# Reordering the first loads, transposes and parameter turns of a one-core encoder layer

## The chip, the cores and the metric

The kernel runs on one core of a Trainium2 chip. The metric is device microseconds of one execution, median of the runs shown. The engines are TensorE (PE, with its weight loads as PEld), VectorE (DVE), ScalarE (ACT), GpSimd (POOL) and SyncE (SP, which here only issues DMAs). ACT also has a DMA queue of its own; the rows call the issuing side of the two queues SPq and ACTq.

## What is computed

Two sequences (512 tokens of width 1024 each) go through one encoder layer with shared weights, in float32:

```python
h = rmsnorm(x, norm1) @ w_in            # 1024 -> 256 + 128 + 32 + 512
# latent attention from the first 416 columns, multi-scale pooling from the last 512
x = x + concat(attn, pool) @ w_out
x = x + (silu(gate) * val) @ w_down     # gate, val = dwconv3(rmsnorm(x, norm2) @ w_up)
x = x + (p @ w_ple_proj) * sigmoid(rmsnorm(x, norm3) @ w_ple_gate + b_ple_gate)
y = rmsnorm(x, final_norm)
```

Only the start of the first line, the input projection, bears on this change.

## The kernel before

Every float32 product is made of three reduced-precision matmuls (`mm3`, L313 to L317): a value v is split into a high part (v rounded) and a low part (v minus the high part), and high by high, high by low and low by high are summed in a PSUM bank. Splitting costs an ACT copy for the high part and a DVE subtraction for the low part, for weights (`split_w_hi` L347 on ACT, `split_w_lo` L353 on DVE) as for activations.

The program is five instruction streams written by hand, one for each engine, tied by semaphores. An engine does its stream in order, so a wait in it holds up all that stands behind.

**The head.** x lies in memory by token and must be turned so that features lie on partitions. SP loads it in eight pieces of 512 KB (`load_x(s, q)`, L420: sequence s, 256 columns, that is features of two units). A unit u is 128 features of one sequence, 16 in all, eight for each sequence; piece q of sequence 0 holds units 2q and 2q + 1. For each unit:

- PE (`x_unit`, L694) makes four 128x128 transposes into one of five PSUM banks (`x_bank`), and counts `x_tr`. From unit 5 on it first waits until unit u - 5 has been read out of its bank.
- ACT (`x_unit`, L1268) writes the high part, scaled by the norm1 gain (L1273, tile XH). For units 1, 3, 5, 7 and 9 (`ACT_TURNED`) it first copies the plain turned x to XT (L1272).
- DVE makes the plain copy of the other eleven units (`x_turned`, L1872) and the low part of all (`x_low`, L1878, tile XL), and counts `x_split`.

The norm1 gain is itself loaded as eight rows (`prow[..., 3, :]`, L1255, ACT's first DMA), turned by one PE transpose (L739, waits for the identity matrix and for norm1) and copied to `par` by DVE (L1865); ACT and DVE need it for every unit. Then PE does eight transposes of the identity into a bank that nobody reads (`unread`, L744), units 0 to 3, 18 more unread transposes, and unit 4.

The weight of the projection is loaded in tiles of 128 columns (`first_in`, `load_in`; WR), whose first tile is also rearranged by two POOL instructions (L2636, L2638) before ACT splits it. With the first tile split, PE runs two loops of eight steps, one for each sequence: step k is the three matmuls of `in_tile(0, s, [k])`, which need low parts up to unit 8s + k, and in the first loop and in three steps of the second also four transposes of a later unit. Steps of the first loop carry units 5 to 12, those of the second 13 to 15. After that the second weight tile is used, whose low part (`split_w_lo(dve, 1, 1)`, L1897) DVE makes after its last `x_low`.

Eleven more small loads (conv taps and bias of 44 rows, gains of 1 to 8 rows) fill `prow`; ACT issues all of them at its very start, ahead of its first activation (L1286, which brings its table load). PE turns them in three transposes (L753, L754, L757) after unit 4, before the first loop; DVE copies them to `par` (L1891, L1892) between units 7 and 8.

Of the kernel before, what the change touches and what calls it, by code (L numbers as in the profile page):

```python
# [25 lines left out]
P = 128  # L26
# [3 lines left out]
KT = D // P  # L30
# [13 lines left out]
N1 = 4 * 2 * FT  # L44
N2, N3, GQ = N1 + KT, N1 + 2 * KT, N1 + 3 * KT
GKV, PSC, BG = GQ + 2, GQ + 3, GQ + 7
NF = BG + KT
NPAR = NF + KT
# [24 lines left out]
ACT_TURNED = (1, 3, 5, 7, 9)  # L73
# [16 lines left out]
def encoder(nc, x, p_in, w, y, consts):  # L90
    with ExitStack() as ctx:
        def sb(name, shape, dt=F32):
            return ctx.enter_context(nc.sbuf_tensor(name, shape, dt))

        def sem(name):
            return ctx.enter_context(nc.semaphore(name))


        par = sb("par", [P, LINE * -(-NPAR // LINE)])
# [6 lines left out]
        ident = sb("ident", [P, P])  # L106
# [22 lines left out]
        prow = XT[:, 4096 - 512:4096].rearrange("p (a d) -> p a d", a=4)  # L129
# [59 lines left out]
        def up_w(v, k):  # L189
# [29 lines left out]
        ps = [ctx.enter_context(nc.psum_tensor(f"ps{b}", [P, 512], F32)) for b in range(8)]  # L219
# [7 lines left out]
        ident_in, norm1_in, gains_in, taps_in, tabs_in, edge_in, row_in = (sem(n) for n in (  # L227
            "ident_in", "norm1_in", "gains_in", "taps_in", "tabs_in", "edge_in", "row_in"))
# [12 lines left out]
        w_hi, w_lo, rot_done = sem("w_hi"), sem("w_lo"), sem("rot_done")  # L241
        consts_set, par_tr, par_copied = sem("consts_set"), sem("par_tr"), sem("par_copied")
# [38 lines left out]
        def slot(n):  # L281
            return (n if n < T_GATE else n + 1) % 2
# [10 lines left out]
        def x_bank(u):  # L293

            return ps[(4, 5, 6, 2, 3)[u % 5]]
# [17 lines left out]
        def mm3(pe, out, wh, wl, xh, xl, first, last, skip=False):  # L313

            pe.matmul(out, wh, xh, start=first, stop=False, skip_group_check=skip)  # L315
            pe.matmul(out, wh, xl, start=False, stop=False, skip_group_check=skip)  # L316
            return pe.matmul(out, wl, xh, start=False, stop=last, skip_group_check=skip)  # L317
# [29 lines left out]
        def split_w_hi(act, n, free, count, cols=KT, base=0):  # L347

            if free is not None:
                act.wait_ge(free, count)  # L350
            act.activation(WH[:, slot(n), base:cols, :], WR[:, slot(n), base:cols, :], ACT.Copy).then_inc(w_hi, 1)  # L351
# [59 lines left out]
        def wtile(v):  # L411
            return v.rearrange("(k p) m -> p k m", p=P)
# [1 line left out]

        @block.sync
        def _(sp):
            sp.dma_start(ident[:, :], consts["ident"]).then_inc(ident_in, 16)
            cols_in = [320, 256, 416 + 3 * P, 416 + 2 * P, 416 + P, 0, None, 128, 416]

            def load_x(s, q):  # L420
                cols = slice(q * 2 * P, (q + 1) * 2 * P)
                sp.dma_start(xtok[s][:, :, cols], x[s].rearrange("(t p) d -> p t d", p=P)[:, :, cols]).then_inc(x_in[s * TT + q], 16)

            def first_in(n):
                sp.dma_start(WR[:, n, :, :], wtile(w["w_in"][:, cols_in[n]:cols_in[n] + P])).then_inc(win_in[n], 16)

            load_x(0, 0)
            load_x(0, 1)
            first_in(0)
            load_x(0, 2)  # L430
            load_x(0, 3)
            load_x(1, 0)
# [252 lines left out]
        def _(pe):  # L685
            def x_unit(u):

                s, f = divmod(u, KT)
                pe.wait_ge(x_in[s * TT + f // 2], 16)
                if u >= 5:  # L690
                    pe.wait_ge(x_split, u - 4)
                b = x_bank(u)
                for t in range(TT):
                    ins = pe.transpose(b[:, t * P:(t + 1) * P], xtok[s][:, t, f * P:(f + 1) * P], ident[:, :])  # L694
                ins.then_inc(x_tr, 1)

            def in_tile(a, s, kts=range(KT), fresh=False):
                n = a + (a >= T_POOL)
                for k in kts:
                    if fresh:  # L700
                        pe.wait_ge(x_split, s * KT + k + 1)
                    ins = mm3(pe, ps[2 * (a % 2) + s][:, :], WH[:, slot(n), k, :], WL[:, slot(n), k, :],
                              XH[:, s, k, :], XL[:, s, k, :], k == 0, k == KT - 1)
                    if k == KT - 1:
                        ins.then_inc(acc_ready, 1)
# [35 lines left out]
            def unread(count):  # L741

                for _ in range(count):
                    pe.transpose(ps[0][:, 0:P], ident[:, :], ident[:, :])  # L744

            unread(8)
            for u in range(4):
                x_unit(u)
            unread(18)
            x_unit(4)  # L750
            pe.wait_ge(taps_in, 16 * 4)
            pe.wait_ge(par_copied, 1)
            pe.transpose(ps[7][:, 0:88], prow[0:88, 0, :], ident[0:88, 0:88])  # L753
# [1 line left out]
            pe.wait_ge(gains_in, 16 * 7)  # L755
            rest = NPAR - N2
            pe.transpose(ps[7][:, 256:256 + rest], prow[0:rest, 2, :], ident[0:rest, 0:rest]).then_inc(par_tr, 1)  # L757
            pe.wait_ge(w_lo, 1)
            for k in range(KT):
                in_tile(0, 0, [k], fresh=True)  # L760
                x_unit(5 + k)
            for k in range(KT):
                in_tile(0, 1, [k], fresh=True)
                if k < 3:
                    x_unit(KT + 5 + k)
            for a in range(1, 8):
                if a == 6:
                    for q in range(4):
# [483 lines left out]
        @block.scalar  # L1252
        def _(act):

            act.dma_start(prow[0:KT, 3, :], w["norm1"].rearrange("(k p) -> k p", p=P)).then_inc(norm1_in, 16)  # L1255
            small = [("norm2", 8), ("norm3", 8), ("q_a_norm", 2), ("kv_a_norm", 1), ("pool_scale", 4),
                     ("b_ple_gate", 8)]
            r = 0
            for name, k in small:
                act.dma_start(prow[r:r + k, 2, :], w[name].rearrange("(k p) -> k p", p=P)).then_inc(gains_in, 16)  # L1260
                r += k
            taps = [w["conv_w"][k] for k in range(3)] + [w["conv_b"]]
            for k in range(4):
                h = (k % 2) * 44
                act.dma_start(prow[h:h + 44, k // 2, :], taps[k].rearrange("(k p) -> k p", p=P)).then_inc(taps_in, 16)
            act.dma_start(prow[r:r + KT, 2, :], w["final_norm"].rearrange("(k p) -> k p", p=P)).then_inc(gains_in, 16)

            def x_unit(u):  # L1268
                s, f = divmod(u, KT)
                act.wait_ge(x_tr, u + 1)  # L1270
                if u in ACT_TURNED:
                    act.activation(xt[:, XS[s], f, :], x_bank(u)[:, :], ACT.Copy)  # L1272
                act.activation(XH[:, s, f, :], x_bank(u)[:, :], ACT.Copy, scale=par[:, N1 + f:N1 + f + 1]).then_inc(x_hi, 1)  # L1273
# [11 lines left out]
            act.wait_ge(consts_set, 1)  # L1285
            act.activation(SF[:, 4096:4097], ones[:, 0:1], ACT.Copy)  # L1286
            act.wait_ge(par_copied, 1)
            for u in range(3):
                x_unit(u)
            act.wait_ge(win_in[0], 16)  # L1290
            act.wait_ge(rot_done, 2)
            split_w_hi(act, 0, None, 0)
            for u in range(3, 2 * KT):
                x_unit(u)
            act.wait_ge(win_in[1], 16)
            split_w_hi(act, 1, None, 0)
            squares(range(ACT_SQUARES))
# [456 lines left out]
            for n in range(4, NU):  # L1754
                down_w(n)
                down_g(n)
                p, k = divmod(n, NPAIR)
# [98 lines left out]
        def _(dve):  # L1856
            def f32(v):
                return v.bitcast(F32)
# [9 lines left out]
            def x_turned(u):  # L1868

                s, f = divmod(u, KT)  # L1870
                dve.wait_ge(x_hi, u + 1)
                dve.tensor_copy(xt[:, XS[s], f, :], x_bank(u)[:, :])  # L1872

            def x_low(u):

                s, f = divmod(u, KT)
                dve.wait_ge(x_hi, u + 1)
                dve.scalar_tensor_tensor(XL[:, s, f, :], x_bank(u)[:, :], par[:, N1 + f:N1 + f + 1],  # L1878
                                         f32(XH[:, s, f, :]), ALU.mult, ALU.subtract).then_inc(x_split, 1)

            for u in range(3):
                if u not in ACT_TURNED:
                    x_turned(u)
                x_low(u)
            split_w_lo(dve, 0, 0)
            for u in range(3, KT):
                if u not in ACT_TURNED:
                    x_turned(u)
                x_low(u)
            dve.wait_ge(par_tr, 2)  # L1890
            dve.tensor_copy(par[:, 0:N1], ps[7][:, 0:N1])  # L1891
            dve.tensor_copy(par[:, N2:NPAR], ps[7][:, 256:256 + NPAR - N2]).then_inc(par_copied, 1)  # L1892
            for u in range(KT, 2 * KT):
                if u not in ACT_TURNED:
                    x_turned(u)
                x_low(u)
# [585 lines left out]
            for n in range(4, NU):  # L2482
                down_wl(n)
                down_gl(n)
                p, k = divmod(n, NPAIR)
# [467 lines left out]
```

## Time and profile before

| | |
|---|---|
| median of 3 runs | 1136.55 us (1134.41 to 1136.68) |
| the profiled execution, its own time | 1135.66 us |
| its span, first to last instruction | 1133.9 us |
| PE busy | 1114.6 us, 98% |
| DVE busy | 831.4 us, 73% |
| ACT busy | 561.8 us, 50% |
| POOL busy | 471.8 us, 42% |

The span is what the trace covers; some 1.8 us of the execution lie around it. Busy shares are over the whole span. PE's 98% includes overlap in its pipeline and the unread transposes, so it says where the bound is and not that nothing can be gained.

### The profile page before, as it was taken

How to read it: one execution, taken by the hardware profiler on the slowest of the kernel's cores; microseconds unless marked ns; L12 is line 12 of the kernel's file. 1: busy time of each engine (PE TensorE's matmuls, PEld its weight loads, DVE VectorE, ACT ScalarE, POOL GpSimd, SP SyncE). 2: the span in 40 equal slices, each digit the busy share in tenths (PEclk: the TensorE clock that was granted, in tenths of full speed). 3: DMA queues.
4: the chain of work that ended last, by engine and by line, in shares of the span. 5: the costliest groups of instructions: out<-in, count | busy, mean ns of one | idle time of the engine just before them, and what ended most of it. 6: DMA issues, size and time to landing. Idle time of an engine off the chain costs nothing.

```text
span 1133.9 us, 15943 instructions
## 1 busy us (share of the span) xinstructions
PE 1114.6 (98%) x5184; PEld 899.0 (79%) x5184; DVE 831.4 (73%) x1168; ACT 561.8 (50%) x991; POOL 471.8 (42%) x409
## 2 busy tenths in 40 slices
PE   8999999999999999999999999999999999999997
PEld 7788766665888877888888888888878888888886
DVE  7895976674469898878787878787866756757565
ACT  6312687775223464444545444454554545634344
POOL 0196642322566046775677567655310201211021
PEclk9999999999999999999999999999999999999999
DMA  6611000104653135444544454445896665534342
GB/s 210 224 30 41 1 12 13 38 19 155 216 193 124 46 121 167 171 134 164 169 168 137 158 175 166 139 159 173 326 331 217 186 204 186 186 94 132 92 138 86
DMA packets 138449, 161.63 MB, mean 143 GB/s; under 512 B 8763, under 2 KB 105370, under 8 KB 133786
## 3 DMA queue, kind: packets, MB, share of 16 engines
q1 hardware_dynamic: 138080, 160.82, 42.6%
q8 instruction: 30, 0.49, 0.2%
q14 instruction: 25, 0.20, 0.1%
q10 hardware_dynamic: 314, 0.11, 0.0%
HBM read 115.56 MB, written 45.35 MB: 142 GB/s over the span
## 4 chain that ended last, share of the span: by engine, by line
PE 83%; DVE 11%; issue 2%; DMA 2%; ACT 1%; POOL 1%; ACTq 0%; DVEq 0%; POOLq 0%
PE ps L315 25%; PE ps L317 25%; PE ps L316 25%; PE ps L893 3%; PE ps L874 2%; DMA WR<-in_w_down 1%; DVE WL L2421 1%; DVE GHL L2425 1%; DMA WR<-t_scratch 1%; DVE SF L2308 1%; PE ps L885 1%; DVE XL L1878 1%; DVE SF L2316 1%; DVE WL L2209 1%; DVE WDHL L2066 1%
## 5 line engine op out<-in xcount | busy, mean ns | idle before, releaser
L315 PE MATMUL ps<-XH,WH 128*128 128x512 f32 (+1 forms) x730 | 285.2, 391 | 3.0 <-DVE WL L2209 1.3
L317 PE MATMUL ps<-XH,WL 128*128 128x512 f32 (+1 forms) x730 | 282.5, 387 | 0.0
L316 PE MATMUL ps<-XL,WH 128*128 128x512 f32 (+1 forms) x730 | 282.4, 387 | 0.0
L315 PEld LDWEIGHTS ps<-XH,WH 128*128 128x128 f32 x730 | 137.1, 188 | 32.7 <-issue 2.5
L317 PEld LDWEIGHTS ps<-XH,WL 128*128 128x128 f32 x730 | 137.0, 188 | 28.2
L316 PEld LDWEIGHTS ps<-XL,WH 128*128 128x128 f32 x730 | 137.2, 188 | 26.9
L315 PE MATMUL ps<-GHL,WH 128*128 128x512 f32 x394 | 153.7, 390 | 1.4 <-DVE WL L2209 0.5
L317 PE MATMUL ps<-GHL,WL 128*128 128x512 f32 x394 | 153.3, 389 | 0.0
L316 PE MATMUL ps<-GHL,WH 128*128 128x512 f32 x394 | 153.3, 389 | 0.0
L351 ACT ACTIVATE WH<-WR 128x1024 fp32r<-128x1024 f32 (+3 forms) x45 | 45.4, 1010 | 121.5 <-PE ps L317 107.2
L1574 ACT ACTIVATE SF<-ps,col 128x512 f32<-128x512 f32 x88 | 68.2, 778 | 73.6 <-PE ps L317 64.1
L2421 DVE TENSOR_TENSOR WL<-WR,WH 128x512 fp32r<-128x512 f32 x77 | 59.2, 769 | 58.8 <-ACT WH L1698 58.6
L1698 ACT ACTIVATE WH<-WR 128x512 fp32r<-128x512 f32 x77 | 48.6, 632 | 93.3 <-PE ps L317 74.0
L2884 POOL TENSOR_TENSOR SF<-SF 128x512 f32<-128x512 f32 x16 | 24.4, 1524 | 167.7 <-ACT SF L1741 167.7
L315 PEld LDWEIGHTS ps<-GHL,WH 128*128 128x128 f32 x394 | 73.9, 188 | 17.7 <-issue 1.6
L317 PEld LDWEIGHTS ps<-GHL,WL 128*128 128x128 f32 x394 | 74.0, 188 | 15.5
L316 PEld LDWEIGHTS ps<-GHL,WH 128*128 128x128 f32 x394 | 74.0, 188 | 15.3
L356 DVE TENSOR_TENSOR WL<-WR,WH 128x1024 fp32r<-128x1024 f32 (+3 forms) x45 | 61.7, 1370 | 26.0 <-ACT WH L351 25.7
L2809 POOL TENSOR_TENSOR XT<-XT 128x512 f32<-128x512 f32 x44 | 69.4, 1577 | 11.8 <-DMA XT<-in_w_down 7.7
L2316 DVE SCALAR_TENSOR_TENSOR SF<-ps,col,SF 128x511 f32<-128x511 f32 x88 | 65.2, 741 | 0.5
L2308 DVE SCALAR_TENSOR_TENSOR SF<-ps,col,SF 128x511 f32<-128x511 f32 x88 | 64.8, 737 | 0.0
L2209 DVE TENSOR_TENSOR WL<-TL,WH 128x512 fp32r<-128x512 f32 x54 | 48.6, 901 | 18.4 <-ACT WH L1530 18.4
(275 smaller groups left out, 2275.9 us busy)
## 6 DMA issues: line engine op xcount, KB each, us to landing
TL<-in_w_up SPq DMA_DIRECT2D x48, 256.0 KB, 3.6
s_scratch<-XT SPq DMA_DIRECT2D x11, 1024.0 KB, 4.7
XT<-in_w_down SPq DMA_DIRECT2D x11, 1024.0 KB, 6.5
t_scratch<-XT SPq DMA_DIRECT2D x11, 1024.0 KB, 3.8
WR<-t_scratch SPq DMA_DIRECT2D x44, 256.0 KB, 3.0
TL<-s_scratch SPq DMA_DIRECT2D x44, 256.0 KB, 3.0
WR<-in_w_up SPq DMA_DIRECT2D x40, 256.0 KB, 3.7
WR<-in_w_down SPq DMA_DIRECT2D x33, 256.0 KB, 3.7
```

The costliest lines, as they stand in the source:

```text
L315: pe.matmul(out, wh, xh, start=first, stop=False, skip_group_check=skip)
L316: pe.matmul(out, wh, xl, start=False, stop=False, skip_group_check=skip)
L317: return pe.matmul(out, wl, xh, start=False, stop=last, skip_group_check=skip)
L351: act.activation(WH[:, slot(n), base:cols, :], WR[:, slot(n), base:cols, :], ACT.Copy).then_inc(w_hi, 1)
L356: dve.tensor_tensor(WL[:, slot(n), base:cols, :], WR[:, slot(n), base:cols, :], WH[:, slot(n), base:cols, :].bitcast(F32), ALU.subtract).t ...
L1574: act.activation(out, ps[4 * f + bank][:, :], ACT.Identity, scale=taps_of(1, val, f), bias=taps_of(3, val, f)).then_inc(tap1, 1)
L1698: act.activation(up_w(WH, d_slot(n)), up_w(WR, d_slot(n)), ACT.Copy).then_inc(w_hi, 1)
L2209: dve.tensor_tensor(up_w(WL, k_slot), raw, f32(up_w(WH, k_slot)), ALU.subtract).then_inc(uw_lo, 1)
L2308: dve.scalar_tensor_tensor(out[:, 1:S], ps[4 * f + bank][:, 0:S - 1], taps_of(0, val, f), out[:, 1:S], ALU.mult, ALU.add).then_inc(tap0, 1)
L2316: dve.scalar_tensor_tensor(out[:, 0:S - 1], ps[4 * f + bank][:, 1:S], taps_of(2, val, f), out[:, 0:S - 1], ALU.mult, ALU.add).then_inc(con ...
L2421: dve.tensor_tensor(up_w(WL, d_slot(n)), up_w(WR, d_slot(n)), f32(up_w(WH, d_slot(n))), ALU.subtract).then_inc(w_lo, 1)
L2809: pool.tensor_tensor(out, a, b, ALU.subtract).then_inc(t_sum, 1)
```

## The change

Five things move. SP no longer loads the identity; ACT does, as its first DMA, ahead of norm1. On SP's queue the first weight tile goes ahead of x's second piece. The other eleven small loads leave ACT's start: the four taps are issued after ACT's units 2 to 5, the seven gains after its units 3 to 9, one of each at a time. PE does units 0 and 1, 16 unread transposes (not 18), units 2 and 3, and then the first loop, which now carries units 4 to 11 (the second carries 12 to 15); the three transposes of the parameters stand between the two loops. On ACT and DVE the first weight tile is split after two units instead of three, and DVE copies the parameters ahead of unit 13 instead of unit 8.

```diff
--- before.py
+++ after.py
@@ -414,7 +414,6 @@
 
         @block.sync
         def _(sp):
-            sp.dma_start(ident[:, :], consts["ident"]).then_inc(ident_in, 16)
             cols_in = [320, 256, 416 + 3 * P, 416 + 2 * P, 416 + P, 0, None, 128, 416]
 
             def load_x(s, q):
@@ -425,8 +424,8 @@
                 sp.dma_start(WR[:, n, :, :], wtile(w["w_in"][:, cols_in[n]:cols_in[n] + P])).then_inc(win_in[n], 16)
 
             load_x(0, 0)
+            first_in(0)
             load_x(0, 1)
-            first_in(0)
             load_x(0, 2)
             load_x(0, 3)
             load_x(1, 0)
@@ -744,10 +743,15 @@
                     pe.transpose(ps[0][:, 0:P], ident[:, :], ident[:, :])
 
             unread(8)
-            for u in range(4):
+            for u in range(2):
                 x_unit(u)
-            unread(18)
-            x_unit(4)
+            unread(16)
+            for u in range(2, 4):
+                x_unit(u)
+            pe.wait_ge(w_lo, 1)
+            for k in range(KT):
+                in_tile(0, 0, [k], fresh=True)
+                x_unit(4 + k)
             pe.wait_ge(taps_in, 16 * 4)
             pe.wait_ge(par_copied, 1)
             pe.transpose(ps[7][:, 0:88], prow[0:88, 0, :], ident[0:88, 0:88])
@@ -755,14 +759,10 @@
             pe.wait_ge(gains_in, 16 * 7)
             rest = NPAR - N2
             pe.transpose(ps[7][:, 256:256 + rest], prow[0:rest, 2, :], ident[0:rest, 0:rest]).then_inc(par_tr, 1)
-            pe.wait_ge(w_lo, 1)
-            for k in range(KT):
-                in_tile(0, 0, [k], fresh=True)
-                x_unit(5 + k)
             for k in range(KT):
                 in_tile(0, 1, [k], fresh=True)
-                if k < 3:
-                    x_unit(KT + 5 + k)
+                if k < 4:
+                    x_unit(KT + 4 + k)
             for a in range(1, 8):
                 if a == 6:
                     for q in range(4):
@@ -1252,18 +1252,22 @@
         @block.scalar
         def _(act):
 
+            act.dma_start(ident[:, :], consts["ident"]).then_inc(ident_in, 16)
             act.dma_start(prow[0:KT, 3, :], w["norm1"].rearrange("(k p) -> k p", p=P)).then_inc(norm1_in, 16)
             small = [("norm2", 8), ("norm3", 8), ("q_a_norm", 2), ("kv_a_norm", 1), ("pool_scale", 4),
                      ("b_ple_gate", 8)]
-            r = 0
-            for name, k in small:
-                act.dma_start(prow[r:r + k, 2, :], w[name].rearrange("(k p) -> k p", p=P)).then_inc(gains_in, 16)
-                r += k
+            small.append(("final_norm", KT))
             taps = [w["conv_w"][k] for k in range(3)] + [w["conv_b"]]
-            for k in range(4):
+
+            def load_gain(j):
+
+                r, k = sum(n for _, n in small[:j]), small[j][1]
+                act.dma_start(prow[r:r + k, 2, :], w[small[j][0]].rearrange("(k p) -> k p", p=P)).then_inc(gains_in, 16)
+
+            def load_taps(k):
+
                 h = (k % 2) * 44
                 act.dma_start(prow[h:h + 44, k // 2, :], taps[k].rearrange("(k p) -> k p", p=P)).then_inc(taps_in, 16)
-            act.dma_start(prow[r:r + KT, 2, :], w["final_norm"].rearrange("(k p) -> k p", p=P)).then_inc(gains_in, 16)
 
             def x_unit(u):
                 s, f = divmod(u, KT)
@@ -1285,13 +1289,17 @@
             act.wait_ge(consts_set, 1)
             act.activation(SF[:, 4096:4097], ones[:, 0:1], ACT.Copy)
             act.wait_ge(par_copied, 1)
-            for u in range(3):
+            for u in range(2):
                 x_unit(u)
             act.wait_ge(win_in[0], 16)
             act.wait_ge(rot_done, 2)
             split_w_hi(act, 0, None, 0)
-            for u in range(3, 2 * KT):
+            for u in range(2, 2 * KT):
                 x_unit(u)
+                if 2 <= u < 6:
+                    load_taps(u - 2)
+                if 3 <= u < 10:
+                    load_gain(u - 3)
             act.wait_ge(win_in[1], 16)
             split_w_hi(act, 1, None, 0)
             squares(range(ACT_SQUARES))
@@ -1878,19 +1886,16 @@
                 dve.scalar_tensor_tensor(XL[:, s, f, :], x_bank(u)[:, :], par[:, N1 + f:N1 + f + 1],
                                          f32(XH[:, s, f, :]), ALU.mult, ALU.subtract).then_inc(x_split, 1)
 
-            for u in range(3):
+            for u in range(2):
                 if u not in ACT_TURNED:
                     x_turned(u)
                 x_low(u)
             split_w_lo(dve, 0, 0)
-            for u in range(3, KT):
-                if u not in ACT_TURNED:
-                    x_turned(u)
-                x_low(u)
-            dve.wait_ge(par_tr, 2)
-            dve.tensor_copy(par[:, 0:N1], ps[7][:, 0:N1])
-            dve.tensor_copy(par[:, N2:NPAR], ps[7][:, 256:256 + NPAR - N2]).then_inc(par_copied, 1)
-            for u in range(KT, 2 * KT):
+            for u in range(2, 2 * KT):
+                if u == KT + 5:
+                    dve.wait_ge(par_tr, 2)
+                    dve.tensor_copy(par[:, 0:N1], ps[7][:, 0:N1])
+                    dve.tensor_copy(par[:, N2:NPAR], ps[7][:, 256:256 + NPAR - N2]).then_inc(par_copied, 1)
                 if u not in ACT_TURNED:
                     x_turned(u)
                 x_low(u)
```

## Rows read from the trace of the kernel before

**Rows 1.** The page, busy time, share and instructions of each engine

```profile
PE 1114.6 (98%) x5184; PEld 899.0 (79%) x5184; DVE 831.4 (73%) x1168; ACT 561.8 (50%) x991; POOL 471.8 (42%) x409
```

**Rows 2.** Chain that ended last, first 30 us: start us, us, what

```profile
5.24 0.35 ACTq L1266
...
7.11 0.59 ACT XH L1273
...
12.25 0.50 PE ps L315
12.74 0.23 PE ps L316
...
13.21 0.44 PE ps L694 x4
...
17.15 0.75 DVE XL L1878
17.90 0.24 DVE par L1891
18.15 0.11 DVE par L1892
...
25.21 0.60 DVE XT L1872
25.81 0.66 DVE XL L1878
...
27.72 1.14 DVE WL L356
...
28.91 0.50 PE ps L315
```

**Rows 3.** Timeline, first 12 us, DMA issues: start us, us, queue, line, what

```profile
0.75 0.61 ACTq L1255 DMA_DIRECT2D XT<-in_norm  x1
0.76 0.38 SPq L417 DMA_DIRECT2D ident<-in_ident  x1
...
1.40 0.68 ACTq L1260 DMA_DIRECT2D XT<-in_norm  x2
```

**Rows 4.** Timeline, first 12 us, PE and ACT around the first tile

```profile
2.78 0.27 PE L739 MATMUL ps<-ident,XT 8*128 8x8 f32 x1 [2.78 <-DMA ident<-in_ident]
...
2.98 1.97 PE L744 MATMUL ps<-ident 128*128 128x128 f32 x8
...
5.18 3.46 PE L694 MATMUL ps<-ident,SF 128*128 128x128 f32 x16 [0.23 <-DMA SF<-in_x_prompt]
...
8.06 1.27 ACT L1273 ACTIVATE XH<-ps,par 128x512 fp32r<-128x512 f32 x2
...
9.00 0.30 POOL L2636 TENSOR_SCALAR WR<-WR 128x128 f32<-128x128 f32 x1 [8.55 <-DMA WR<-in_w_in]
...
9.63 1.06 ACT L351 ACTIVATE WH<-WR 128x1024 fp32r<-128x1024 f32 x1 [0.30 <-POOL WR L2638]
...
11.51 0.25 PE L757 MATMUL ps<-ident,XT 39*128 39x39 f32 x1
```

**Rows 5.** DMA issues, single loads by window of issue: KB, us to landing

```profile
SF<-in_x_prompt SPq DMA_DIRECT2D x1, 512.0 KB, 3.9
ident<-in_ident SPq DMA_DIRECT2D x1, 64.0 KB, 2.0
...
WR<-in_w_in SPq DMA_DIRECT2D x1, 512.0 KB, 6.7
```

**Rows 6.** Windows 18 to 22 us: busy by engine, clock, DMA share, GB/s

```profile
18.00:20.00 2.00, 2.00 (x14) 1.65 (x13) 2.00 (x5) 1.78 (x3) 0.00 (x0) 1.00 0.62 186
20.00:22.00 2.00, 2.00 (x15) 1.75 (x13) 2.00 (x5) 1.11 (x3) 0.00 (x0) 1.00 0.00 0
```

**Rows 7.** Windows 368 to 374 us, the same columns

```profile
368.00:370.00 2.00, 2.00 (x16) 1.88 (x16) 0.16 (x1) 0.00 (x0) 0.45 (x1) 1.00 0.88 246
370.00:372.00 2.00, 2.00 (x7) 1.55 (x6) 1.36 (x4) 0.00 (x0) 0.57 (x1) 0.52 1.06 307
372.00:374.00 2.00, 2.00 (x7) 1.55 (x6) 0.78 (x2) 0.00 (x0) 0.00 (x0) 0.62 0.45 136
```

## The prediction

> **What bounds the kernel now.** I read the page first: PE is busy for 1114.6 us, 98% of the span [rows 1], so what can be won lies where PE waits. The change is in the head, so the next view is the chain that ended last, over the first 29 us [rows 2]. It runs ACT's DMA issues, ACT's table load, ACT's first high part (7.11), then DVE, to PE's first projection matmul at 12.25; and at the end DVE's low part of the second weight tile (27.72), which PE needs to go on at 28.91. That last number is the one to predict: behind it PE runs with few waits, so a shift of 28.91 is taken as the shift of the end.
>
> Two things in the chain matter. Before 12.25 the head is a chain of latencies. From unit 7's low part (17.15) to 28.91 the chain stays on DVE without a gap, save its last hand-over: 0.75 for that low part, 0.24 + 0.11 for the parameters, then copies of 0.60 and low parts of 0.66, then 1.14 [rows 2]. From unit 10 on a unit costs DVE 1.26, more than a step of PE's loop: 3 x 0.23 + 0.44 = 1.13 [rows 2]. PE supplies the units up to 7, DVE paces the rest.
>
> **The change, part by part.**
>
> *New first matmul.* Before, ACT could not start until its last small issue ended at 5.59 [rows 2]. Moved away, they leave 2 on ACT, and what follows them there, table load and first activation (5.59 to 7.11, 1.5 us), ends near 3.3, so ACT is no longer what is late. Next late is the gain of norm1: its load was ACT's first issue (0.75) and is now the second, where the old second began, 1.40 [rows 3]. When it lands the trace does not print. From below: PE's norm1 transpose ran at 2.78 [rows 4], so the old load took at most 2.03, which gives 3.43. From above: 3.9, as the first x piece took [rows 5], gives 5.3. It is 4 KB, and nearest in size is the identity, 64 KB in 2.0 [rows 5]; but the x piece now enters at 0.76 rather than behind the identity and runs beside both. I take 2.5, landing at 3.9.
>
> [...]
>
> From 3.9: PE's norm1 transpose 0.2 (2.78 to 2.98), eight unread transposes 1.97, and eight of units 0 and 1 at half of 3.46, with a little added because the second half ran faster: 1.8 [rows 4]. That is 7.87. The x piece does not hold this up: issued at 0.76 with 3.9, it lands at 4.7 [rows 3, 5], ahead of PE at 6.07. Then on ACT unit 1's plain copy and high part, 1.2 together (two such instructions took 1.27), and the weight's high part, 1.06 [rows 4]; on DVE the weight's low part, 1.14 [rows 2]; hand-overs 0.15: 11.4, against 12.25. The weight tile itself is no obstacle: issued about 1.2 in place of the second piece, it lands by 8 even with its old 6.7 [rows 5], POOL's 0.6 (its start at 9.00 to ACT's at 9.63 [rows 4]) brings 8.6, and ACT is ready for it at 9.1. That is the edit of SP's queue: it hides, and would cost only from 0.5 us later. The second x piece moves to the tile's old place, landing about 8.9; PE wants it after 16 unread transposes, past 9, so this costs nothing. The 16 for 18 unread ones lie in the wait for the weight.
>
> *A longer loop.* Units are now one step deeper: unit 7 is turned in the fourth step instead of the third. Unit 7's low part starts 4.90 after the first matmul before (17.15 - 12.25), 4.90 + 1.13 = 6.03 after. That gives 11.4 + 6.03 = 17.43, which is 0.28 later than 17.15: the 0.85 won in front is spent.
>
> *DVE behind it.* The parameters (0.35) no longer stand between units 7 and 8. That wins nothing: unit 9 is turned at 11.4 + 1.4 + 5 x 1.13 = 18.45, ACT's copy and high part put its low part at 19.7, and DVE, without the parameters, is free 0.33 before. Before, the copies filled just this gap. They come back in front of unit 13 with the full 0.35. And PE's three parameter transposes, about 0.4 (the last alone 0.25 [rows 4]), now stand between the loops and delay unit 12 by 0.16 against DVE. Sum: 0.28 + 0.33 + 0.16 = 0.77. The second pass starts at 29.7 instead of 28.9.
>
> *Small loads between ACT's units.* Eleven issues of about 0.35 [rows 2] now stand behind the activations of units 2 to 9. Queued behind each is ACT's next unit, and behind that DVE and PE. I price this at nothing: ACT has two high parts of 0.67 in 1.27 [rows 4], so the next one is under way before the last has ended, and an issue should run beside an activation. If the cover is gone, see the second rival. The last gain is issued after unit 9, near 18.9; PE wants all of them at about 11.4 + 9.5 = 20.9. DMA traffic ends in 18 to 20 us (62%, then 0) [rows 6], so a load in that lull takes about the identity's 2.0 and lands at 20.9: just in time. From above: the old last issue, at 5.24 [rows 2], was there when PE turned it at 11.51 [rows 4], so 6.3 us at most, which would cost 4.3.
>
> **Sum.** Against the profiled execution (1135.66, of which 1133.9 is span): +0.8, 1136.4. That execution is 0.89 below the median of 1136.55, which gives 1137.3 for the median. A measurement can tell about 0.2%, 2.3 us, from no change; this is 0.07%. *Forecast: no difference that can be told.* With norm1's bounds, 3.43 and 5.3, the same sum is +0.3 and +2.2.
>
> **The rivals.**
>
> *Latency won in front carries through (faster).* If identity and norm1 came as early as before, PE would start at 2.78, the first matmul stand at 10.3, and the shift be 10.3 - 11.4 + 0.8 = -0.3; with transposes of 0.11 [rows 2] instead of 0.22 for units 0 and 1 another 0.9 is won, -1.2. Against it: traffic until near 20 us [rows 6]. A last gain that lands at 20.3 puts unit 12 at 21.75, DVE's copy of it at 22.45, and the rest (0.60 + 0.66 + 0.35 + 3 x 1.26 + 1.14 + hand-over) at 29.0, no gain at all. So 1135.3 to 1136.6.
>
> *The small issues block ACT (slower).* One mechanism: ACT does not issue a DMA while an activation runs. Then units 3, 4 and 5 are followed by 0.7 each and 2 and 6 to 9 by 0.35. ACT's own work is 1.2 for units with a plain copy and 0.67 for the others; with 0.7 added that is over PE's 1.13, and ACT falls behind by 1.8 us, ending unit 9 at 21.4. The last gain is issued then, lands at 23.8 instead of 20.9, PE waits 2.8 between the loops, and DVE with it: 0.8 + 2.8 = +3.6, 1140.2. It decides from an issue cost of some 0.25 on ACT. For it: the trace has no issue between activations on any engine that computes. Against it: the overlap of 1.27 for two [rows 4]. In the Trainium skill, Advanced Engine Details and Errata, section Engine Queue Depths, ScalarE on trn2 holds 8 instructions in its queue; by that the issues would go on beside activations. No row here shows it.
>
> *PE's granted clock moves (either way).* From 370 to 374 us the granted clock was 0.52 and 0.62 of full, so PE was in part at the lower of its two levels, 1.2 GHz instead of 2.4; in the 2 us before it fell, PE did 16 short matmuls with its weight loads at 1.88 of 2 us [rows 7]. What was not granted is (0.48 + 0.38) x 2 = 1.7 us. A shifted head may lose such a stretch or gain another: 1135.6 or 1139.0 with the shift. The three runs, 2.3 us apart, could hold both.
>
> **How the numbers follow.** Forecast 0.60; faster rival 0.15, mostly within 0.2% by its own price; blocked ACT 0.14, all beyond 0.2%; clock 0.11, split. Faster by over 0.2% needs the best of the first rival and a lost stretch of low clock: 0.05. Slower by over 0.2%: the blocked ACT and part of the clock case on top of a late norm1, 0.16. Within: 0.79. Range: from a shift of 0.2 with the clock's 1.7 won, 1135.0, through the late norm1 (+2.2, 1138.8) to that with 1 us of waiting for the small loads, 1139.8; the blocked ACT lies above it and is the part left out.
>
> **What would show it.** Right: first projection matmul near 11.4, norm1's transpose past 3.4, DVE idle before unit 9's low part, parameters ahead of unit 13, second pass at 29 to 30.5. Wrong: a first matmul before 10.3 (the latency chain is misread); ACT idle-free with gaps at the issues and PE waiting over 1 us between the loops (the second rival); the second pass before 28.5, which would mean that DVE did not pace the end of the head.

## The result, and the profile after

| | before | after |
|---|---|---|
| median, 22 runs each | 1136.38 us | 1138.04 us |
| ratio | | 1.0018, 95% interval 1.0012 to 1.0024 |
| span of the profiled execution | 1133.9 us | 1137.4 us |
| PE's norm1 transpose | 2.78 | 5.40 |
| first projection matmul | 12.25 | 12.51 |
| second pass | 28.91 | 30.89 |

The change made the kernel slower: by 0.18% or 2.05 us by the ratio, by 1.66 us if the two medians are subtracted. That is just inside the 0.2% that the forecast called no difference; the forecast itself was 0.8 us. "Second pass" is PE's start on the second weight tile. Its shift in the profile, 30.89 - 28.91 = 1.98, is as large as that.

The chain that ended last, changed kernel, first 31 us (start us, us, what):

```profile
1.24 4.03 DMA XT<-in_norm
5.27 0.14 issue
5.40 0.24 PE ps L738
5.64 1.90 PE ps L743 x8
7.54 0.87 PE ps L693 x4
...
8.50 0.70 ACT XH L1277
...
9.29 0.69 DVE XT L1880
9.98 1.32 DVE XL L1886 x2
11.30 1.17 DVE WL L356
...
12.51 0.50 PE ps L315
...
23.51 0.70 ACT XH L1277
...
24.23 0.69 DVE XT L1880
...
29.70 1.14 DVE WL L356
30.84 0.04 issue
30.89 0.50 PE ps L315
```

Where ACT's issues led the chain of [rows 2], the load of norm1 leads now: issued at 1.24, landed at 5.27, 4.03 us later. PE cannot start before it. The identity, now on ACT's queue too, took 3.6 instead of the 2.0 of [rows 5], and x's first piece 4.3. DMA issues of the changed kernel by windows of issue (KB, us to landing):

```profile
SF<-in_x_prompt SPq DMA_DIRECT2D x1, 512.0 KB, 4.3
ident<-in_ident ACTq DMA_DIRECT2D x1, 64.0 KB, 3.6
...
WR<-in_w_in SPq DMA_DIRECT2D x1, 512.0 KB, 5.3
```

The timeline of the changed kernel from 15 to 25 us (start us, us, engine, line, what, idle before and what ended it):

```profile
15.08 0.60 ACT L1276 ACTIVATE XT<-ps 128x512 f32<-128x512 f32 x1 [0.45 <-PE ps L693]
15.09 0.30 ACTq L1270 DMA_DIRECT2D XT<-in_conv_b  x1
15.42 0.29 ACTq L1265 DMA_DIRECT2D XT<-in_q_a_norm  x1
...
17.35 0.60 ACT L1276 ACTIVATE XT<-ps 128x512 f32<-128x512 f32 x1 [0.44 <-PE ps L693]
...
18.55 0.75 DVE L1886 SCALAR_TENSOR_TENSOR XL<-ps,par,XH 128x512 fp32r<-128x512 f32 x1 [0.26 <-ACT XH L1277]
...
20.81 0.75 DVE L1886 SCALAR_TENSOR_TENSOR XL<-ps,par,XH 128x512 fp32r<-128x512 f32 x1 [0.25 <-ACT XH L1277]
...
21.90 0.25 PE L761 MATMUL ps<-ident,XT 39*128 39x39 f32 x1
...
24.23 0.69 DVE L1880 COPY XT<-ps 128x512 f32<-128x512 f32 x1 [0.16 <-ACT XH L1277]
```

Two small loads are issued while ACT's copy of unit 5 runs, and ACT's next idle time (0.44) is again ended by PE: the issues cost ACT nothing. They stand behind unit 5 in ACT's program and still start with its first instruction. The low parts of units 7 (18.55) and 9 (20.81) and the copy of unit 12 (24.23) come with the small waits that the prediction had put there. The last parameter transpose (21.90) waits for no load.

The span of the profiled execution grew by 3.5 us, more than the time over all runs. The 1.5 beyond the second pass's 1.98 fall behind 55 us: this one execution has a second stretch of low clock, beside one like that of [rows 7]. Windows of the changed kernel, PE alone (busy, granted clock, DMA share, GB/s):

```profile
54.00:56.00 2.00, 1.75 (x16) 1.00 0.66 183
56.00:58.00 2.00, 2.00 (x7) 0.52 0.27 79
58.00:60.00 2.00, 2.00 (x7) 0.62 0.00 0
60.00:62.00 2.00, 2.00 (x10) 1.00 0.30 91
```

In the same place, behind the 16 short matmuls of the pool squares' sums, the profiled execution before had kept its clock. Over many runs the mean granted clock is the same, 0.9969 in the 22 of the changed kernel and 0.9969 in the 33 of the kernel before that ran beside e1 to e4, so this does not explain the 2.05.

### The profile page after: what moved, and what is told of

Its sections match the earlier page's. It is cut to its first block, busy times and chain, and to the rows that moved or that the text cites. A ratio compares the mean times of both kernels' runs of the same rounds, so it can differ in the third digit from the quotient of the medians.

```text
span 1137.4 us, 15939 instructions
## 1 busy us (share of the span) xinstructions
PE 1115.2 (98%) x5182; PEld 899.1 (79%) x5182; DVE 831.6 (73%) x1168; ACT 561.8 (49%) x991; POOL 471.2 (41%) x409
## 4 chain that ended last, share of the span: by engine, by line
PE 83%; DVE 10%; DMA 2%; issue 2%; ACT 1%; POOL 1%; DVEq 0%; POOLq 0%; ACTq 0%
PE ps L315 25%; PE ps L317 25%; PE ps L316 25%; PE ps L893 3%; PE ps L874 2%; DMA WR<-in_w_down 1%; DVE WL L2426 1%; DVE GHL L2430 1%; DVE SF L2313 1%; DMA WR<-t_scratch 1%; PE ps L885 1%; DVE SF L2321 1%; DVE WL L2214 1%; DVE WDHL L2071 1%; DVE col L2082 1%
```

## The experiments

Twelve kernels ran, each 8 to 12 times beside runs of the kernel before on the same chip. "Sums" in the table is the start of PE's 16 short matmuls near 52 us; they stand 23.35 to 23.50 us behind the second pass in all rows but e7 (23.82) and e11 (24.00). All but the ratio are from one profile of each.

| kernel | norm1 turned | first matmul | second pass | sums | ratio to before (95%) |
|---|---|---|---|---|---|
| before | 2.78 | 12.25 | 28.91 | 52.26 | 1 |
| changed | 5.40 | 12.51 | 30.89 | 54.24 | 1.0018 (1.0012 to 1.0024) |
| e1 identity on SP | 2.63 | 10.47 | 29.67 | 53.03 | 1.0005 (0.9995 to 1.0014) |
| e2 identity alone moved | 5.24 | 13.67 | 30.32 | 53.69 | 1.0013 (1.0004 to 1.0022) |
| e3 norm1 first | 5.87 | 13.21 | 31.58 | 54.95 | 1.0022 (1.0013 to 1.0030) |
| e4 x waits for norm1 | 2.83 | 12.22 | 31.07 | 54.42 | 1.0022 (1.0012 to 1.0032) |
| e5 e1, turns late | 2.68 | 10.45 | 28.59 | 51.94 | 0.9996 (0.9986 to 1.0005) |
| e6 e5, two copies to ACT | 2.59 | 10.28 | 27.88 | 51.34 | 0.9999 (0.9989 to 1.0009) |
| e7 before, two copies to ACT | 2.61 | 12.33 | 28.48 | 52.30 | 1.0001 (0.9991 to 1.0010) |
| e8 e1, unit 4 ahead | 2.61 | 11.91 | 28.88 | 52.38 | 0.9994 (0.9985 to 1.0003) |
| e9 e5, tile third | 2.68 | 11.20 | 29.31 | 52.68 | 1.0010 (1.0001 to 1.0018) |
| e10 e5, small loads first | 2.68 | 10.83 | 28.96 | 52.33 | 1.0012 (1.0003 to 1.0021) |
| e11 e6, spread later | 2.63 | 11.25 | 28.83 | 52.83 | 0.9999 (0.9991 to 1.0008) |
| e12 e6, few unread | 2.66 | 10.83 | 28.46 | 51.92 | 0.9999 (0.9989 to 1.0009) |

**e1: the identity back on SP's queue.**

```diff
-            act.dma_start(ident[:, :], consts["ident"]).then_inc(ident_in, 16)
...
+            sp.dma_start(ident[:, :], consts["ident"]).then_inc(ident_in, 16)
             cols_in = [320, 256, 416 + 3 * P, 416 + 2 * P, 416 + P, 0, None, 128, 416]
```

> The changed kernel with the identity back on SP's queue (first there) and norm1 again ACT's first load; all else stays changed. Theory (the late norm1 gain is what costs; the rest of the change is near zero): PE's norm1 transpose is back at 2.8, the first projection matmul comes at 10.2 to 10.6 and the second pass at 28.6 to 29.2, so the time is that of the kernel before within 0.4 us, some 2 us under the changed kernel. Rival (the deeper loop and the parameter turns between the loops cost by themselves): the second pass stays near 30.9 although the first matmul is early, and the time stays about 2 us above the kernel before.

The ratio falls to 1.0005, which is no difference from the kernel before. The first matmul comes where the theory has it, 2.04 earlier than in the changed kernel, but the second pass only 1.22 earlier, 29.67 instead of 28.6 to 29.2. So the theory holds for most of the 2 us, and 0.82 of the gain is lost on the way. PE's waits of e1 up to 45 us (us in total, times, longest) say where:

```profile
PE ps L739 <- DMA ident<-in_ident: 2.6, 1, 2.6
PE ps L762 <- DMA XT<-in_final_norm: 0.7, 1, 0.7
```

The second is the parameter transpose between the loops, which waits for the last small load: issued at 17.59, it let PE go on at 20.68.

**e2: that move alone, on the kernel before.**

```diff
-            sp.dma_start(ident[:, :], consts["ident"]).then_inc(ident_in, 16)
             cols_in = [320, 256, 416 + 3 * P, 416 + 2 * P, 416 + P, 0, None, 128, 416]
...
+            act.dma_start(ident[:, :], consts["ident"]).then_inc(ident_in, 16)
             act.dma_start(prow[0:KT, 3, :], w["norm1"].rearrange("(k p) -> k p", p=P)).then_inc(norm1_in, 16)
```

> The kernel before with one edit of the change: the identity goes from SP's queue to the front of ACT's. Theory: norm1 lands past 5 instead of by 2.8, the first high part moves from 7.0 to about 8.5, the first matmul from 12.25 to about 13.7, and the second pass by 1.3 to 1.7: 1.3 to 1.7 us slower than before. Rival (ACT's own late start at 7.0 hides the late gain): under 0.5 us slower.

Second pass +1.41, ratio 1.0013, 1.5 us (0.5 to 2.5): the theory. Chain of e2:

```profile
1.24 3.87 DMA XT<-in_norm
...
5.48 1.90 PE ps L743 x8
7.38 3.41 PE ps L693 x16
10.79 2.18 PE ps L743 x18
...
13.74 0.43 PE ps L315
```

Here norm1 took 3.87, and from then on PE's own row of transposes sets the first matmul; in the kernel before ACT's start at 7.11 had been later than PE's first unit.

**e3 and e4: why norm1 lands late.** e3 issues norm1 ahead of the identity; e4 holds x's first piece until norm1 has landed.

```diff
+            act.dma_start(prow[0:KT, 3, :], w["norm1"].rearrange("(k p) -> k p", p=P)).then_inc(norm1_in, 16)
             act.dma_start(ident[:, :], consts["ident"]).then_inc(ident_in, 16)
-            act.dma_start(prow[0:KT, 3, :], w["norm1"].rearrange("(k p) -> k p", p=P)).then_inc(norm1_in, 16)
```

> The changed kernel with ACT's first two loads in the other order: norm1, then the identity. Theory (a small load waits behind the x piece that SP issued ahead of it, whichever load it is): norm1 lands by 3, the identity past 4, PE starts at 4.5 to 5.5 instead of 5.4, and the time is 0 to 1 us under the changed kernel. Rival (only a second issue on ACT's queue with few rows is slow, the wide identity load is not): PE starts near 3.4 and the time is 1.5 to 2 us under the changed kernel.

```diff
+            sp.wait_ge(norm1_in, 16)
             load_x(0, 0)
```

> The changed kernel with SP's first load of x held until norm1 has landed. Theory (norm1 is late because its packets share the DMA engines with x): without x in flight norm1 lands 1.4 to 2.0 after its issue at 1.24, so by 3.3, and PE's norm1 transpose moves from 5.4 to 2.8 to 3.4; x's first piece then lands near 7 and the first matmul stands near 12, the second pass at 30 to 30.6. Rival (the ACT queue is slow with its second load by itself): norm1 still lands near 5.3 and everything behind x is about 4 us later.

Heads of the chains, e3:

```profile
0.75 0.62 ACTq L1255
1.36 0.04 issue
1.40 4.42 DMA ident<-in_ident
```

and e4:

```profile
1.18 1.51 DMA XT<-in_norm
2.69 0.02 issue
2.71 3.57 DMA SF<-in_x_prompt
```

In e3 the identity takes the place of the late load, 4.42 instead of norm1's 4.03, and PE starts at 5.87, later than the 4.5 to 5.5 that the theory gave; the second pass is 0.69 later than the changed kernel's and the ratio 1.0022 against 1.0018: not the gain of the rival, nor the 0 to 1 us under it of the theory. In e4, with no x in flight and only the identity's 64 KB beside it, the same norm1 load at the same place in ACT's queue lands in 1.51. That speaks against a second issue on ACT that is slow by itself: x in flight is what makes it late. That agrees with the Trainium skill, DMA: Bandwidth & Descriptors, section Issuing engines are not separate DMA queues: loads of different engines run on the same 16 DMA engines and interleave. Whether the DMA engines or the memory behind them hold norm1 up, no run here separates.

e4 is as slow as the changed kernel all the same, and its second pass, 31.07, missed the expected 30 to 30.6. x is not the reason: its first transposes stand at 6.32, about 1 us earlier than in the changed kernel. But the 16 unread transposes behind them took 3.52 instead of 1.91, so that the first matmul is only 0.29 earlier, and the last small load, issued at 19.31, holds PE for 0.4 between the loops.

**e5: the parameters turned later.** On e1; the three transposes go behind unit 15, DVE's copies ahead of unit 15.

```diff
             for k in range(KT):
                 in_tile(0, 1, [k], fresh=True)
                 if k < 4:
                     x_unit(KT + 4 + k)
+                if k == 3:
+                    pe.wait_ge(taps_in, 16 * 4)
...
-                if u == KT + 5:
+                if u == 2 * KT - 1:
                     dve.wait_ge(par_tr, 2)
```

> The changed kernel with the identity back on SP's queue, and the three parameter transposes moved from between PE's two loops to behind unit 15 in the second loop (DVE's copies go ahead of unit 15). Theory (with norm1 early, the last small load, landing at 20.6, is what PE waits for between the loops): no wait there, unit 12 is turned 1.0 us earlier, and the second pass starts at 28.4 to 28.9 with a first matmul at 10.5, so 0 to 0.5 us under the kernel before and about 1 us under the variant with the turns between the loops. Rival (the longer loop alone gives the 2 us back): second pass at 29.5 or later.

Second pass at 28.59, 1.08 earlier than e1 with the same first matmul (10.45 and 10.47); ratio 0.9996 after 1.0005. So the turns between the loops, 0.7 of waiting and 0.3 for the three transposes, were what held e1 back. Chain of e5:

```profile
18.76 0.75 DVE XL L1887
19.51 0.60 DVE XT L1881
...
27.40 1.14 DVE WL L356
28.54 0.04 issue
28.59 0.50 PE ps L315
```

From 18.76 it is DVE alone.

**e9 and e10: the two parts of the change that help.** On e5; e9 puts the first weight tile behind x's second piece again, e10 all small loads at ACT's start.

```diff
             load_x(0, 0)
-            first_in(0)
             load_x(0, 1)
+            first_in(0)
```

> The variant with the identity on SP's queue and the parameters turned behind unit 15, but with the first weight tile behind x's second piece again, as before the change. Theory (with norm1 early the weight tile is the next thing late): it lands near 8.9, ACT splits it at 9.6, the first matmul moves from 10.5 to 11.8 to 12.1 and the second pass from 28.6 to 29.8 to 30.2: 1.2 to 1.6 us slower than the variant with the tile second, 0.9 to 1.3 slower than the kernel before. Rival (the tile's place in the queue is hidden either way): both stay within 0.3.

```diff
+            for j in range(6):
+                load_gain(j)
+            for k in range(4):
+                load_taps(k)
+            load_gain(6)
             act.wait_ge(consts_set, 1)
...
-                if 2 <= u < 6:
-                    load_taps(u - 2)
-                if 3 <= u < 10:
-                    load_gain(u - 3)
```

> The variant with the identity on SP's queue and the parameters turned behind unit 15, but with all small loads issued at ACT's start again, as before the change. Theory (without them ACT waits for PE, with them PE's units wait for ACT's first activation at 7.0): first high part at 7.0 to 7.2 instead of 6.3, first matmul at 11.0 to 11.3, second pass at 29.1 to 29.5: 0.5 to 0.8 us slower than the variant with them between the units. Rival (they cost as much between the units as at the start): no difference.

e9: second pass 0.72 later than e5, less than the 1.2 to 1.6 expected, because the tile landed at 8.1 rather than 8.9; the ratio, 1.0010 against 0.9996, gives 1.6 but with an interval of about 1 us on each. e10: 0.37 later, and 1.0012 in the ratio, again more than its profile shows. Both directions are the theory's; the sizes in the profiles are under those expected (1.2 to 1.6, 0.5 to 0.8), and the ratios are good only to about a microsecond. Chain of e9, the weight now leading:

```profile
2.21 5.91 DMA WR<-in_w_in
8.12 0.08 issue
8.20 0.30 POOL WR L2642
```

**e8: unit 4 ahead of the first loop.** On e1.

```diff
+            x_unit(4)
             for k in range(KT):
                 in_tile(0, 0, [k], fresh=True)
-                x_unit(4 + k)
+                x_unit(5 + k)
...
-                if k < 4:
-                    x_unit(KT + 4 + k)
+                if k < 3:
+                    x_unit(KT + 5 + k)
```

> The changed kernel with the identity back on SP's queue, and unit 4 turned ahead of the first loop again (loops carry units 5 to 12 and 13 to 15, as before). Theory (the deeper loop costs one step of 1.13 in front of DVE's unbroken stretch): PE waits for x's third piece near 10.7, the first matmul comes later, at 11.0 to 11.4, but unit 7's low part comes earlier, near 16.1 instead of 16.5; unit 12 no longer waits for the small loads; second pass at 28.0 to 28.5, 0.4 to 0.9 us under the kernel before. Rival (an earlier first matmul is what counts): the second pass is later than with unit 4 in the loop, 29.7 or more.

Second pass 28.88: 0.79 better than e1 though its first matmul, 11.91, is 1.44 later. So the rival falls. But e8 differs from e1 in two things, since its unit 12 is turned ahead of the parameters and does not wait for the small loads. Against e5, which lacks that wait too, the way from the first matmul to the second pass is 1.17 shorter (16.97 instead of 18.14), about the one step of 1.13, while the second pass itself is 0.29 later. The 28.0 to 28.5 was missed with a first matmul expected by 11.4: the chain runs over PE's 16 unread transposes, which took twice as long as in e5. Chain of e8:

```profile
7.41 3.41 PE ps L744 x16
10.82 0.47 PE ps L694 x4
...
12.04 0.69 DVE XT L1881
...
28.88 0.50 PE ps L315
```

From 12.04 to the second pass it is DVE alone.

**e6, e7, e11, e12: is there a version that beats both?** e6 and e7 give ACT the plain copies of units 11 and 13, on e5 and on the kernel before (first edit below); e11 puts two matmuls of `spread` (L734 and L735, which need a diagonal, CHL, from DVE) two steps later in the second pass of e6 (second); e12 is e6 with 4 unread transposes instead of 16 (third).

```diff
-ACT_TURNED = (1, 3, 5, 7, 9)
+ACT_TURNED = (1, 3, 5, 7, 9, 11, 13)
...
-                        in_tile(a, s, range(3 if s else 2))
+                        in_tile(a, s, range(5 if s else 2))
                         spread(B_X + 1 - s, 5 - s)
-                        in_tile(a, s, range(3 if s else 2, KT))
+                        in_tile(a, s, range(5 if s else 2, KT))
...
-            unread(16)
+            unread(4)
```

> The variant with the identity on SP's queue and the parameters turned behind unit 15, and the plain copies of units 11 and 13 moved from DVE to ACT. Theory (DVE paces the end of the head): DVE loses 2 x 0.60, the second pass starts at 27.3 to 27.9, where PE's two loops themselves end, and the time is 1.0 to 1.6 us under the kernel before. Rival (ACT, which has 0.44 free in each unit there, becomes late): second pass at 28.4 or later, no gain over the variant without this.

> The kernel before with one edit: the plain copies of units 11 and 13 are made by ACT instead of DVE. Theory (DVE paces the end of the head before the change too): first matmul stays at 12.25, the second pass moves from 28.9 to 27.9 to 28.2, 0.7 to 1.0 us faster than before. Rival (the first matmul sets the end): second pass stays at 28.9.

> The variant with the identity on SP's queue, late parameters and the copies of units 11 and 13 on ACT, and one more edit: in the second pass PE does the two spreading matmuls after five steps of the second sequence instead of three. Theory (the gain at the second pass, 1.0 us, goes through to the pool squares' wait at 52 in the kernel before, and more of it once PE does not wait at the spread): that wait ends 1.0 to 1.4 us earlier than before and the time is 1.0 to 1.4 us under the kernel before. Rival (something behind the head takes the gain): no difference from before, as the variant without this edit seemed to show (ratio 0.9999).

> The variant with the identity on SP's queue, late parameters and the copies of units 11 and 13 on ACT, with 4 unread transposes between units 1 and 2 instead of 16. The 16 took 1.9 us in some executions and 3.6 in others, and where they took long PE reached the first matmul after the weight was split. Theory (in those executions the unread transposes themselves hold up the first matmul): first matmul at 10.2 to 10.7 in every execution, second pass near 27.9, the sums at 51.2 to 51.6, and a time 0.5 to 1.2 us under the kernel before. Rival (fewer unread transposes leave PE slow for longer, so its first loop runs at half rate for some steps): transposes and matmuls of the first steps take twice as long, and the time is that of the kernel before or more.

e6's profile has what was expected up to the sums, 0.92 earlier than before, yet its ratio is 0.9999 (0.9989 to 1.0009): the interval holds the gain and holds nothing. e7 missed: its second pass moved by 0.43 and at the sums nothing was left. PE's waits of e7 name the place, a wait at the spread that the kernel before does not have:

```profile
PE ps L734 <- DVE CHL L1916: 0.2, 1, 0.2
```

That is DVE's diagonal, which hangs on ACT's five rows of squares. In e7 ACT begins these at 26.61, as in the kernel before (26.53), so an earlier second pass runs into them; in e6 ACT begins at 25.66, and only 0.11 is lost up to the sums. e11 was to avoid the wait at the spread. Its execution began late (first matmul 11.25, the 16 unread transposes 3.20 in the timeline), and its edit put another wait in the place:

```profile
PE ps L315 <- DVE SF L1948: 0.4, 1, 0.4
```

From the second pass to the sums e11 takes 24.00 us instead of e6's 23.46, so in this profile the later spread does not help. e12 came with x's first piece landing at 5.35 and a first matmul at 10.83, outside its 10.2 to 10.7, with no step of its first loop at half rate; so its rival falls, but no gain shows. No variant is shown to beat the kernel before. e5, e6, e8, e11 and e12 are no slower than it by more than 0.1%, as the upper ends of their intervals say.

## Why the prediction was right, and which term was too small

The range (1135.0 to 1139.8) held, and the predicted 1137.3 was 0.7 under the measured 1138.04. The case, no difference that can be told, held narrowly: with 22 runs each the interval excludes no change at all, and it is the forecast's limit of 0.2% that 0.18% stays under. Two of the prediction's own signs of being right failed: the first matmul came at 12.51 and not near 11.4, the second pass at 30.89, past its 29 to 30.5. The other three (norm1's transpose past 3.4, DVE idle before unit 9's low part, the parameters ahead of unit 13) are in the rows above. Step by step:

- **norm1's landing** is the term that was mis-sized. Taken: 2.5 us after the issue, at 3.9. Measured: 4.03, at 5.27. The row that it was taken nearest to, the identity in 2.0 [rows 5], was for a load issued 0.43 ahead of x; in this change x goes 0.48 ahead of norm1. The upper bound, x's own 3.9, was the right neighbour: with 5.3 the prediction's sum gave +2.2, measured +1.98 at the second pass and 2.05 by the ratio.
- **From there to the first matmul**: 7.5 forecast (3.9 to 11.4), 7.24 measured (5.27 to 12.51). The sum agrees, the path only in part: the forecast ran over ACT's split of the weight, the chain runs over DVE's copy of unit 0 and its two low parts (9.29 to 11.30). ACT's split ended at 11.20, so either way gives nearly the same time, which the forecast did not foresee.
- **The longer loop**: unit 7's low part at 6.03 behind the first matmul, measured 18.55 - 12.51 = 6.04. e8, which takes that step back, agrees (1.17 against e5), though DVE and not the loop paces it.
- **DVE behind it**: idle 0.33 before unit 9 forecast, 0.25 measured; 0.16 before unit 12, measured 0.16. From the first matmul to the second pass 18.3 forecast, 18.38 measured.
- **Small issues at no cost on ACT**: right, the issue at 15.09 runs beside the copy at 15.08. That is what the 8 places in ScalarE's queue (the Trainium skill, Advanced Engine Details and Errata, Engine Queue Depths) would give; the row shows it.
- **The small loads' landing just in time**: right for the changed kernel, no wait at 21.90. That was luck, owed to the late norm1: the last load was issued at 19.61, when the DMA share had fallen (0.21 from 19 to 20 us). In e1, with PE 2 us earlier, it was issued at 17.59 with the share still full (1.11 and 1.06 from 17 to 19 us) and was late, until 20.68, as the first rival had it (20.3).
- **The tile ahead and the small loads moved** help, by 0.72 (e9) and 0.37 (e10) in the profiles, with norm1 early; in the changed kernel, where norm1 is late, no run prices them.

Of the rivals, the faster one is answered by e1: with the identity early the first matmul does come 1.8 us earlier than before, and none of it is left in the time: the second pass stands at 29.67, later still than the 29.0 that the rival had for a late last load. The blocked ACT did not happen. The clock stretch did, in the profile, without a bias over the runs.

So the shift of 1.98 splits along the chain, between the rows of the kernel before and of the changed one. The first matmul is 0.26 later (forecast: 0.85 earlier), the way from there to unit 7's low part 1.14 longer (forecast 1.13), the way from there to the second pass 0.58 longer (forecast 0.49), of which DVE's idle 0.25 and 0.16 are the larger part. Only the first term was off, through norm1's landing.

The identity's move by itself costs about 1.4 (e2), or 1.2 when it is taken back (e1). What is then left, 0.76 at the second pass of e1, is less than the 1.08 that turning the parameters later wins (e5); the ratio of e1 alone does not tell it from nothing.

## What to carry to other kernels

At a kernel's start, issue the loads that the first instruction needs ahead of the big ones, as the kernel before does: here a 4 KB load issued half a microsecond behind a 512 KB one took 4 us instead of 1.5, and another engine's queue did not protect it. Holding the big load back until the small one had landed (e4) brought no gain. Price such a load by the big transfer that is in flight beside it, not by a small one that went ahead. And when a latency is cut in front of a saturated stretch, find what paces that stretch first (here DVE, from unit 7 on), and what was in time only because all was late (here the parameters).

## What the runs showed of the hardware

- *Load latency under load.* norm1, 4 KB: 4.03 and 3.87 issued 0.48 behind x (changed kernel, e2), 1.51 with only the identity beside it (e4). The identity, 64 KB: 2.0 issued 0.43 ahead of x, 3.6 issued with it (changed kernel), 4.42 issued 0.64 behind it (e3).
- *PE's first microseconds differ between executions.* Sixteen unread transposes after unit 1 took 1.91 us in the changed kernel and in e5, 3.62 in e8, about half the rate. That would fit the lower of the two clock levels (1.2 instead of 2.4 GHz), but the granted clock reads 1.00 in both stretches, so no row shows it. The three slowest, e4 (3.52), e8 (3.62) and e11 (3.20), are those in which PE had stood idle longest before its first transposes of x: 1.35, 0.65 and 0.87 us, against 0.24 in e5. There PE and not the weight set the first matmul, 0.2 to 1.1 us after DVE had split the weight. Timeline rows of e5 and of e8:

```profile
6.81 1.91 PE L744 MATMUL ps<-ident 128*128 128x128 f32 x16
```

```profile
7.20 3.62 PE L744 MATMUL ps<-ident 128*128 128x128 f32 x16
```

- *Much of the spread between runs is the clock.* Of the 33 runs of the kernel before beside e1 to e4, those at a mean granted clock of 0.996 averaged 1136.9 us, those at 0.998 1134.4; in the three later sets of runs the two were 1.2 to 2.0 us apart. In the profiles the fall stands at two places, behind the sums (54 to 62 us) and near 370 us: the changed kernel has both, e1 the first, e6 the second, e4 neither. From the sums to the end the profiles with neither took 1080.7 us on average (3 of them), with one 1081.6 (8), with both 1083.1 (3), so a fall costs some 1.2 us, nearly as much as this change, and single runs cannot judge it.
